# A third seven-product unit in the first output pair of the second MLP product, groups 0 to 2

## The chip, the cores and the metric

The kernel runs on one core of a Trainium2 chip. Its time is the device time of one execution in microseconds (us), as the median of several runs. The engines are TensorE (PE, matrix products; PEld is its weight load), VectorE (DVE), ScalarE (ACT), GpSimd (POOL) and SyncE (SP), which issues the loads of the weights.

## The reference

One encoder layer on 256 tokens with a width of 2048, in float32. The change lies in its last part, the MLP:

```
h2 = rms_norm(x, g_mlp[layer])
x = x + jnp.square(jax.nn.relu(h2 @ w_mlp_in[layer])) @ w_mlp_out[layer]
...
return rms_norm(x, g_final)
```

`w_mlp_in` is 2048 x 8192 and `w_mlp_out` 8192 x 2048. The hidden values are computed and used in four groups (`g` 0 to 3) of 2048 columns.

## The kernel before, in words

**Precision.** Every float32 operand is split into a high part (`whi`, rounded by ScalarE, `high_part`, L637) and a low part (`wlo`, what is left, by VectorE, `low_part`, L1022). One product in float32 is then three products on TensorE: high by high, high by low, low by high (`three_passes`, L1719 to L1721). A *block* is one such pair of parts, made of one piece of weights of 128 x 1024 elements.

**Loads.** SyncE loads the pieces in the order in which they are used (L610) into seven slots in this stage (`raw`, and part of `gates`). A slot is loaded again when the low part of the last block that needs it has been made (`released`).

**A group.** Four strips of hidden values (`hidden`, j = 0 to 3) come out of the first product. Of each, VectorE adds two halves (L1472), takes the maximum with 0 and scales (L1474), ScalarE squares (L938) and rounds to `b_hi` (L941), VectorE makes `b_lo` (L1479). This is done beside TensorE's next window. Then comes the second product, which has four strips of 512 output columns, two at a time: `pair(g, 0)` and `pair(g, 1)` (group 3 has the first pair only). I call them pair 0 and pair 1. A pair runs over four *units* of 512 hidden values, with four pieces each.

**Plain and crossed units.** The hidden values of a unit are 2 x 2 tiles (halves of the tokens by halves of the unit), and so are its weights (halves of the unit by the two strips): eight tile products in a plain unit. A crossed unit does the same with seven products of sums and differences (`seven`, the Winograd form of Strassen's rule). For it VectorE makes four sums of hidden values (`s_sum`, L1485 to L1490), split into `s_hi` (ScalarE, L944) and `s_lo` (VectorE, L1493), once a unit; and four differences of weight pieces (L1025), in place. The seven blocks are b11, b22, t1, b21, t3, t2, t4, in this order; b11, b22 and b21 are pieces as loaded, t1 to t4 differences. So a plain unit has four blocks with 12 products of 512 columns each on TensorE, a crossed one seven blocks with 6 each.

**Which units are crossed.** Before the change: units 1 and 2 in pair 0, units 0, 1 and 2 in pair 1 (`CROSSED`). The sums are there for the hidden strips 0 to 2 (`SUMMED`).

**PSUM.** It has two halves, G and S, with four banks each. In pair 0 the plain units and three of the seven products add up in G (`sums_bank`), the other four of the seven in S (`mix_bank`); in pair 1 it is the other way round. So before pair 1 begins, ScalarE has to copy pair 0's S banks out (`mix_out`, L967, done in the order of its work at step `MIX_OUT` of the pair's second half), and TensorE waits for that (`m_out`). G is copied at the start of pair 1 (`carry_out`, L954).

**What sets the order.** Each engine works through its list in program order. A table written at build time (`DUE`) says at which step of TensorE's pieces each block is split: about seven blocks ahead. High parts also wait until the block eight places back has been used (`slot_free`), low parts for their high part, and TensorE for the low part (`lo_made`).

Of the kernel before, what the change touches and what calls it, by code (L numbers as in the profile page):

```python
# [66 lines left out]
def walk(eng, window):  # L67
# [36 lines left out]
    for g in range(4):  # L104
# [20 lines left out]
PAIR_ORDER = {  # L125
    0: tuple((unit, part) for unit in range(4) for part in range(4)),
    1: ((3, 0), (3, 1), (0, 0), (0, 1), (0, 2), (0, 3), (1, 0), (1, 1), (1, 2), (1, 3), (3, 2), (2, 0), (2, 1), (2, 2),
        (2, 3), (3, 3)),
}
MIX_OUT = {0: 4, 1: 5}  # L130
# [7 lines left out]
def pair_place(n):  # L138

    g, i = divmod(n - N_MLP, 8 * PIECES)  # L140
    if n < N_MLP or i < 4 * PIECES or (g == 3 and i >= 6 * PIECES):
        return None
    q, i = divmod(i - 4 * PIECES, 2 * PIECES)
    return (g, q) + PAIR_ORDER[q][i]


def crossed(n):

    at = pair_place(n)
    return at is not None and at[2] in CROSSED[at[1]]  # L150


def crossed_before(g, q, unit):

    return g * (len(CROSSED[0]) + len(CROSSED[1])) + q * len(CROSSED[0]) + CROSSED[q].index(unit)


def piece_slot(n):
# [103 lines left out]
def build(nc, x, x_t, w_in, w_dt, gains_in, taps_in, rows_in, w_ssm_up, w_attn_up, w_out, w_mlp_in, w_mlp_out,  # L262
# [275 lines left out]

    def pair_done(g, q, unit):

        return BLOCK[N_MLP + 8 * PIECES * g + 4 * PIECES + 2 * PIECES * q + PAIR_ORDER[q].index((unit, 3)) + 1]

    cum_rows = nc.dram_tensor("cum_rows", (2, HEADS, T), F32).ap()

# [87 lines left out]
    def _(act):  # L632
# [294 lines left out]
        def hidden(p, idx, pr, pp):  # L927
            g, j = idx
            if p == 0:
                act.wait_ge(used, done(pr, pp))  # L930
                if g or j > SUMMED[0]:
                    act.wait_ge(s_lo_made, len(SUMMED) * g + sum(u < j for u in SUMMED))
# [9 lines left out]
            if p == 5 and j in SUMMED:  # L942
                act.wait_ge(s_v, 4 * (len(SUMMED) * g + j) + 4)
# [11 lines left out]

        def mix_out(p, idx, pr, pp):
            g, q = idx
            if p != MIX_OUT[q]:
                return
            act.wait_ge(used, pair_done(g, q, CROSSED[q][-1]))  # L960
# [58 lines left out]
    def _(dve):  # L1019
# [445 lines left out]
        def hidden(p, idx, pr, pp):  # L1465
            g, j = idx
            if p == 0:
                dve.wait_ge(hid_t, g * 4 + (j + 1))
                if 4 * g + j:
                    dve.wait_ge(hid_lo, g * 4 + j)  # L1470
                dve.wait_ge(hid_hi, g * 4 + (j + 1))
                dve.tensor_tensor(hidden_u, hidden_t, hidden_banks(j)[:, :, 0:T], ALU.add).then_inc(h_taken, 1)  # L1472
                dve.wait_ge(h_taken, g * 4 + (j + 1))
                dve.scalar_tensor_tensor(out=hidden_u, in0=hidden_u, scalar=0.0,  # L1474
                                         in1=rstd_row[:, :].unsqueeze(1).to_broadcast([P, 4, T]),
                                         op0=ALU.max, op1=ALU.mult).then_inc(hid_v, 1)
            if p == 2:
                dve.wait_ge(hid_hi, g * 4 + (j + 2))
                dve.tensor_tensor(b_lo[:, 4 * j:4 * j + 4, :], hidden_u,  # L1479
                                  b_hi[:, 4 * j:4 * j + 4, :].bitcast(F32), ALU.subtract).then_inc(hid_lo, 1)  # L1480
            if p == 3 and j in SUMMED:
                a11, a12 = hidden_u[:, 0:2, 0:P], hidden_u[:, 2:4, 0:P]
                a21, a22 = hidden_u[:, 0:2, P:T], hidden_u[:, 2:4, P:T]
                turn = 4 * (len(SUMMED) * g + j)
# [6 lines left out]
            if p == 5 and j in SUMMED:  # L1491
                dve.wait_ge(s_hi_made, len(SUMMED) * g + j + 1)
# [220 lines left out]
    def _(pe):  # L1713
# [230 lines left out]
        def seven(block, q, unit, m, start, stop):  # L1944
# [5 lines left out]
            if block in ("b11", "t2", "t3", "t1"):  # L1950
                first_one, last_one = start, stop
            else:
                first_one, last_one = False, (block, q, unit) == ("b22", 1, 2)
# [12 lines left out]
        def pair_window(r, par, idx):  # L1966

            g, q, _ = idx
            turn = 2 * g + q
            for p in range(PIECES):  # L1970
                n = piece_number(r, par, p)
                _, _, unit, part = pair_place(n)
                if (unit, part) == PAIR_ORDER[q][0]:
                    if q:
                        pe.wait_ge(m_out, 2 * turn)
                    else:
                        pe.wait_ge(h_taken, 4 * g + 3)
                        pe.wait_ge(hid_lo, 4 * g + 3)
                if (unit, part) == (CROSSED[q][0], 0):
                    pe.wait_ge(s_lo_made, len(SUMMED) * (g + 1))  # L1980
                    if q:
                        pe.wait_ge(c_out, 2 * (g + 1))
                    else:
                        pe.wait_ge(h_taken, 4 * g + 4)
                if (q, unit, part) == (0, 3, 0):
                    pe.wait_ge(hid_lo, 4 * g + 4)
                if crossed(n):
                    for i in range(2 * part, min(2 * part + 2, len(PAIR_BLOCKS))):
                        pe.wait_ge(lo_made, BLOCK[n] + i + 1)
# [183 lines left out]
```

## Time and profile before

| | us |
|---|---|
| median of 3 runs (1622.16 to 1622.67) | 1622.39 |
| span of the profiled execution, first to last instruction | 1620.0 |
| TensorE busy in it | 1608.5 |
| VectorE busy | 1264.1 |
| ScalarE busy | 917.1 |

The profiled execution is one execution; its rows give durations and the order of events, and its span lies 2.4 us under the median of the runs. An engine's busy time is averaged over stages that differ, so the pairs are to be read by themselves.

### The profile page before, as it was taken

How to read it: one execution, taken by the hardware profiler on the slowest of the kernel's cores; microseconds unless marked ns; L12 is line 12 of the kernel's file. 1: busy time of each engine (PE TensorE's matmuls, PEld its weight loads, DVE VectorE, ACT ScalarE, POOL GpSimd, SP SyncE). 2: the span in 40 equal slices, each digit the busy share in tenths (PEclk: the TensorE clock that was granted, in tenths of full speed). 3: DMA queues.
4: the chain of work that ended last, by engine and by line, in shares of the span. 5: the costliest groups of instructions: out<-in, count | busy, mean ns of one | idle time of the engine just before them, and what ended most of it. 6: DMA issues, size and time to landing. Idle time of an engine off the chain costs nothing.

```text
span 1620.0 us, 20751 instructions
## 1 busy us (share of the span) xinstructions
PE 1608.5 (99%) x8104; PEld 1362.2 (84%) x8104; DVE 1264.1 (78%) x1520; ACT 917.1 (57%) x1262; POOL 79.1 (5%) x67
## 2 busy tenths in 40 slices
PE   9999999999999999999999999999999999999998
PEld 7888888888888888888888888888888888888886
DVE  7888878888666677776665576999799988998893
ACT  6666556666565445544444555665556556655562
POOL 3000000000001134000000000000000000000000
PEclk9999999999999999999999999999999999999999
DMA  7666665666556664445576676458646764586471
GB/s 272 202 200 190 189 200 189 208 195 203 183 186 182 191 187 153 142 145 175 187 229 195 225 236 187 144 182 285 184 125 224 262 190 134 194 282 209 148 245 53
DMA packets 134194, 312.21 MB, mean 193 GB/s; under 512 B 9744, under 2 KB 10448, under 8 KB 133968
## 3 DMA queue, kind: packets, MB, share of 16 engines
q1 hardware_dynamic: 129376, 302.21, 58.4%
q10 hardware_dynamic: 4720, 8.68, 2.0%
q8 instruction: 64, 1.05, 0.3%
q14 instruction: 34, 0.28, 0.0%
HBM read 308.68 MB, written 2.16 MB: 192 GB/s over the span
## 4 chain that ended last, share of the span: by engine, by line
PE 96%; DVE 2%; issue 1%; ACT 0%; POOL 0%; DMA 0%; POOLq 0%; DVEq 0%
PE G L1719 17%; PE G L1720 17%; PE G L1721 17%; PE G L1728 13%; PE S L1728 7%; PE G L1732 6%; PE S L1719 4%; PE S L1721 4%; PE S L1720 4%; PE S L1732 4%; PE S L1740 1%; PE S L1847 1%; DVE wlo L1022 1%; PE S L1891 0%; PE S L1824 0%
## 5 line engine op out<-in xcount | busy, mean ns | idle before, releaser
L637 ACT ACTIVATE whi<-raw 128x1024 fp32r<-128x1024 f32 x395 | 417.0, 1059 | 418.1 <-PE G L1721 254.9
L1022 DVE TENSOR_TENSOR wlo<-raw,whi 128x1024 fp32r<-128x1024 f32 x395 | 482.5, 1236 | 128.7 <-ACT whi L637 127.4
L1719 PE MATMUL G<-whi,a_both 128*128 128x512 f32 x768 | 301.3, 392 | 2.3 <-DVE wlo L1022 1.7
L1721 PE MATMUL G<-whi,a_both 128*128 128x512 f32 x768 | 299.5, 390 | 0.0
L1720 PE MATMUL G<-wlo,a_both 128*128 128x512 f32 x768 | 299.5, 390 | 0.0
L1728 PE MATMUL G<-a_both,whi 128*128 128x512 f32 x640 | 201.7, 397 | 0.0
L1719 PEld LDWEIGHTS G<-whi,a_both 128*128 128x128 f32 x768 | 144.3, 188 | 33.3 <-issue 2.6
L1721 PEld LDWEIGHTS G<-whi,a_both 128*128 128x128 f32 x768 | 144.2, 188 | 30.1
L1720 PEld LDWEIGHTS G<-wlo,a_both 128*128 128x128 f32 x768 | 144.3, 188 | 28.7
L1732 PEld LDWEIGHTS G<-a_both,wlo 128*128 128x128 f32 x640 | 120.3, 188 | 28.2
L1719 PE MATMUL G<-whi,b_hi 128*128 128x512 f32 x342 | 133.9, 392 | 0.0
L1720 PE MATMUL G<-wlo,b_hi 128*128 128x512 f32 x342 | 133.6, 391 | 0.0
L1721 PE MATMUL G<-whi,b_lo 128*128 128x512 f32 x342 | 133.3, 390 | 0.0
L637 ACT ACTIVATE whi_late<-raw 128x1024 fp32r<-128x1024 f32 x85 | 88.9, 1058 | 67.2 <-PE S L1732 22.0
L1732 PE MATMUL G<-a_both,wlo 128*128 128x256 f32 x640 | 125.9, 278 | 0.0
L1022 DVE TENSOR_TENSOR wlo_late<-raw,whi_late 128x1024 fp32r<-128x1024 f32 x85 | 102.6, 1221 | 24.7 <-ACT whi_late L637 24.1
L637 ACT ACTIVATE whi_late<-gates 128x1024 fp32r<-128x1024 f32 x67 | 70.0, 1056 | 49.7 <-PE G L1732 17.9
L1728 PEld LDWEIGHTS G<-a_both,whi 128*128 128x128 f32 x640 | 97.6, 189 | 0.1
L1022 DVE TENSOR_TENSOR wlo_late<-gates,whi_late 128x1024 fp32r<-128x1024 f32 x67 | 81.1, 1221 | 18.7 <-ACT whi_late L637 18.6
L637 ACT ACTIVATE whi<-gates 128x1024 fp32r<-128x1024 f32 x63 | 66.2, 1056 | 38.2 <-PE G L1732 13.9
L1022 DVE TENSOR_TENSOR wlo<-gates,whi 128x1024 fp32r<-128x1024 f32 x63 | 76.3, 1222 | 12.5 <-ACT whi L637 12.0
L1728 PE MATMUL G<-a_both,whi_late 128*128 128x512 f32 x256 | 80.5, 396 | 0.0
(306 smaller groups left out, 2692.4 us busy)
## 6 DMA issues: line engine op xcount, KB each, us to landing
raw<-in_w_in SPq DMA_DIRECT2D x208, 512.0 KB, 4.3
raw<-in_w_mlp_in SPq DMA_DIRECT2D x74, 512.0 KB, 4.0
raw<-in_w_mlp_out SPq DMA_DIRECT2D x74, 512.0 KB, 5.0
gates<-in_w_mlp_in SPq DMA_DIRECT2D x54, 512.0 KB, 4.0
gates<-in_w_mlp_out SPq DMA_DIRECT2D x54, 512.0 KB, 4.9
raw<-in_w_ssm_up SPq DMA_DIRECT2D x32, 512.0 KB, 3.8
raw<-in_w_attn_up SPq DMA_DIRECT2D x32, 512.0 KB, 4.6
raw<-in_w_out SPq DMA_DIRECT2D x32, 512.0 KB, 4.6
```

Of the source, the lines that this page charges most:

```text
L637: act.activation(high(m), piece(n), ACT.Copy).then_inc(hi_made, 1)
L1022: dve.tensor_tensor(low(m), piece(n), high(m).bitcast(F32), ALU.subtract).then_inc(lo_made, 1)
L1719: pe.matmul(out_ap, hi[:, k, cols], w_hi, start=start, stop=False)
L1720: pe.matmul(out_ap, hi[:, k, cols], w_lo, start=False, stop=False)
L1721: return pe.matmul(out_ap, lo[:, k, cols], w_hi, start=False, stop=stop)
L1728: pe.matmul(banks[:, c, :], high(m)[:, cols[kk]], a_both[:, 2 * p + kk, :, :].rearrange("p h t -> p (h t)"), start=(p + kk == 0), stop=False)
L1732: last = pe.matmul(banks[:, c, 0:T], low(m)[:, cols[kk]], a_hi[:, 2 * p + kk, :], start=False, stop=(2 * p + kk == KT - 1))
L1740: last = pe.transpose(S[:, c // 2, c % 2 * T + tb * P:c % 2 * T + (tb + 1) * P], src(c, tb), ident[:, :])
L1847: last = pe.matmul(S[:, 2, (4 * c + h) * HD:(4 * c + h + 1) * HD], mw[:, 0, h, c, :], tm[:, c, h * HD:(h + 1) * HD], start=True, stop=True)
```

## The change

In groups 0 to 2, pair 0 gets a third crossed unit: units 1, 2 and 3, with unit 0 plain. The fourth hidden strip gets its sums, `s_hi` and `s_lo` too; they are put into the scratch tiles `tmp_b` and `tmp_a`. Pair 0's pieces now come in pair 1's pattern: half of the plain unit, two crossed units, a quarter of the plain unit, the third crossed unit, the last quarter. Pair 0's copies (`mix_out`) move from step 4 to step 5 and behind the first split of that step, as in pair 1. Group 3 stays as it was. The core of the diff:

```diff
-CROSSED = {0: (1, 2), 1: (0, 1, 2)}
-SUMMED = (0, 1, 2)
...
+def summed(g):
+    return (0, 1, 2) if g == LAST_GROUP else (0, 1, 2, 3)
...
+def crossed_units(g, q):
+
+    if g == LAST_GROUP:
+        return (1, 2)
+    return (0, 1, 2) if q else (1, 2, 3)
...
+    if g == LAST_GROUP:
+        return whole(0) + whole(1) + whole(2) + whole(3)
+    plain = 3 if q else 0
+    u, v, w = crossed_units(g, q)
+    return ((plain, 0), (plain, 1)) + whole(u) + whole(v) + ((plain, 2),) + whole(w) + ((plain, 3),)
...
+def mix_step(g):
+    return 4 if g == LAST_GROUP else 5
...
-    cut = 1 if at is not None and at[1] == 1 and s % PIECES == MIX_OUT[1] else 0
+    cut = 1 if at is not None and at[0] < LAST_GROUP and s % PIECES == mix_step(at[0]) else 0
...
+    s_hi.append(nc.alloc_sbuf_tensor_at("s_hi3", [P, 4, 2, P], F32R, offset=region_t))
+    s_lo.append(nc.alloc_sbuf_tensor_at("s_lo3", [P, 4, 2, P], F32R, offset=region_t - 4 * TB * N))
...
-            if p == 3 and j in SUMMED:
+            if p == 3 and j in summed(g):
...
-                if (unit, part) == (CROSSED[q][0], 0):
-                    pe.wait_ge(s_lo_made, len(SUMMED) * (g + 1))
+                if (unit, part) == (units[0], 0):
+                    pe.wait_ge(s_lo_made, 4 * g + 3)
...
                 if (q, unit, part) == (0, 3, 0):
                     pe.wait_ge(hid_lo, 4 * g + 4)
+                    if unit in units:
+                        pe.wait_ge(s_lo_made, 4 * g + 4)
```

How it moves the work on VectorE, in pair 0 of group 0, from the addition of the fourth hidden strip on (`tmp_b<-tmp_a,S`). `wlo` and `wlo_late` are low parts, rows that write `raw` or `gates` the differences. Before:

```order
L1472 TENSOR_TENSOR tmp_b<-tmp_a,S 128x1024
L1474 SCALAR_TENSOR_TENSOR tmp_b<-tmp_b,rstd_row 128x1024
L1022 TENSOR_TENSOR wlo<-raw,whi 128x1024 x2
L1479 TENSOR_TENSOR b_lo<-tmp_b,b_hi 128x1024
L1022 TENSOR_TENSOR wlo<-gates,whi 128x1024 x2
L1025 TENSOR_TENSOR gates<-gates 128x1024
L1022 TENSOR_TENSOR wlo_late<-raw,whi_late 128x1024
L1025 TENSOR_TENSOR gates<-raw,gates 128x1024
L1022 TENSOR_TENSOR wlo_late<-gates,whi_late 128x1024
L1025 TENSOR_TENSOR raw<-raw,gates 128x1024
L1022 TENSOR_TENSOR wlo_late<-raw,whi_late 128x1024
```

After (the same operations stand 24 lines lower in the file: L1046 is L1022, L1049 is L1025, L1496 to L1503 are L1472 to L1479), up to the last difference of the pair's second unit:

```order
L1496 TENSOR_TENSOR tmp_b<-tmp_a,S 128x1024
L1498 SCALAR_TENSOR_TENSOR tmp_b<-tmp_b,rstd_row 128x1024
L1046 TENSOR_TENSOR wlo<-raw,whi 128x1024 x2
L1049 TENSOR_TENSOR raw<-gates,raw 128x1024
L1046 TENSOR_TENSOR wlo<-gates,whi 128x1024
L1503 TENSOR_TENSOR b_lo<-tmp_b,b_hi 128x1024
L1049 TENSOR_TENSOR gates<-gates 128x1024
L1046 TENSOR_TENSOR wlo<-raw,whi 128x1024
L1049 TENSOR_TENSOR gates<-gates,raw 128x1024
L1046 TENSOR_TENSOR wlo_late<-gates,whi_late 128x1024
L1049 TENSOR_TENSOR gates<-gates 128x1024
```

and right behind it, with the sums of the fourth strip (L1509 to L1514) and its low part (L1517):

```order
L1509 TENSOR_TENSOR tmp_a<-tmp_b 128x256
L1510 TENSOR_TENSOR tmp_a<-tmp_b 128x256
L1512 TENSOR_TENSOR tmp_a<-tmp_a,tmp_b 128x256
L1514 TENSOR_TENSOR tmp_a<-tmp_b,tmp_a 128x256
L1046 TENSOR_TENSOR wlo_late<-gates,whi_late 128x1024 x3
L1517 TENSOR_TENSOR s_lo_134<-tmp_a,s_hi_133 128x1024
```

The strip's two first operations stood behind the fourth of the first unit's seven blocks and now stand behind the sixth (the two low parts that follow are t3 and t2 before, t4 and the next unit's b11 after); `b_lo` is now among the second unit's blocks. The four sums and `s_lo` are new at this place.

On ScalarE, around its copies of pair 0's S banks (`mt<-S`), with the semaphores that each row waits for (`landed` with a number is the slot of the load). Before:

```order
L637 ACTIVATE whi_late<-gates 128x1024 [waits used,landed6]
L637 ACTIVATE whi_late<-raw 128x1024 [waits used,landed0]
L637 ACTIVATE whi<-raw 128x1024 [waits used,landed1]
L967 ACTIVATE mt<-S 128x1024 [waits used]
L967 ACTIVATE mt<-S 128x1024
L637 ACTIVATE whi<-raw 128x1024 [waits used,landed3]
L637 ACTIVATE whi<-raw 128x1024 [waits used,t_made]
```

After:

```order
L661 ACTIVATE whi<-gates 128x1024 [waits used,landed6]
L661 ACTIVATE whi<-raw 128x1024 [waits used,landed0]
L661 ACTIVATE whi<-raw 128x1024 [waits used,landed1]
L661 ACTIVATE whi_late<-raw 128x1024 [waits used,landed3]
L991 ACTIVATE mt<-S 128x1024 [waits used]
L991 ACTIVATE mt<-S 128x1024
L661 ACTIVATE whi_late<-raw 128x1024 [waits used,t_made]
L661 ACTIVATE whi_late<-gates 128x1024 [waits used,landed4]
```

The high part ahead of the copies was that of b11 of pair 1's first unit (`landed1`) and is now that of its b22 (`landed3`), which came behind the copies before.

## Rows read from the trace of the kernel before

In timelines a row has: start (us from the span's start), duration (of the merged rows together), engine, line, operation, out<-in, shapes, count, and in brackets the idle time before it with what ended it.

**Rows 1.** Page: busy time of an engine, chain that ended last

```profile
PE 1608.5 (99%) x8104; PEld 1362.2 (84%) x8104; DVE 1264.1 (78%) x1520; ACT 917.1 (57%) x1262; POOL 79.1 (5%) x67
PE 96%; DVE 2%; issue 1%; ACT 0%; POOL 0%; DMA 0%; POOLq 0%; DVEq 0%
```

**Rows 2.** Busy time of each engine in pair 0 and pair 1 of group 0

```profile
core 0: us, PE busy (x) PEld busy (x) DVE busy (x) ACT busy (x) POOL busy (x), PEclk, DMA share, GB/s
1019.67:1060.48 40.81, 40.81 (x182) 33.80 (x181) 37.71 (x33) 26.98 (x27) 0.00 (x0) 1.00 0.54 180
1060.48:1099.92 39.44, 39.44 (x175) 32.67 (x174) 37.59 (x33) 26.57 (x27) 0.00 (x0) 1.00 0.60 193
```

**Rows 3.** Timeline of TensorE: where the stretches start, and one block

```profile
1019.67 0.40 PE L1719 MATMUL G<-whi,b_hi 128*128 128x512 f32 x1
...
1060.48 0.39 PE L1719 MATMUL S<-whi_late,b_hi 128*128 128x512 f32 x1
...
1093.12 0.39 PE L1719 MATMUL G<-whi,s_hi 128*128 128x512 f32 x1
...
1099.92 0.39 PE L1728 MATMUL G<-a_both,whi_late 128*128 128x512 f32 x1
```

**Rows 4.** Timeline of VectorE in pair 1 of group 0

```profile
1067.28 1.23 DVE L1022 TENSOR_TENSOR wlo_late<-gates,whi_late 128x1024 fp32r<-128x1024 f32 x1 [1.31 <-ACT whi_late L637]
1068.61 1.23 DVE L1025 TENSOR_TENSOR gates<-gates 128x1024 f32<-128x1024 f32 x1
...
1076.75 1.22 DVE L1022 TENSOR_TENSOR wlo<-gates,whi 128x1024 fp32r<-128x1024 f32 x1
1077.89 4.63 DVE L1022 TENSOR_TENSOR wlo_late<-raw,whi_late 128x1024 fp32r<-128x1024 f32 x4
...
1090.77 1.22 DVE L1022 TENSOR_TENSOR wlo<-gates,whi 128x1024 fp32r<-128x1024 f32 x1
```

**Rows 5.** Timeline of VectorE around the start of pair 0

```profile
1007.10 1.23 DVE L1022 TENSOR_TENSOR wlo<-gates,whi 128x1024 fp32r<-128x1024 f32 x1 [0.31 <-ACT whi L637]
1008.24 0.42 DVE L1485 TENSOR_TENSOR tmp_a<-tmp_b 128x256 f32<-128x256 f32 x1
...
1009.88 1.22 DVE L1022 TENSOR_TENSOR wlo<-raw,whi 128x1024 fp32r<-128x1024 f32 x1
1012.66 1.23 DVE L1022 TENSOR_TENSOR wlo_late<-raw,whi_late 128x1024 fp32r<-128x1024 f32 x1 [1.56 <-ACT whi_late L637]
...
1021.03 1.23 DVE L1022 TENSOR_TENSOR wlo_late<-gates,whi_late 128x1024 fp32r<-128x1024 f32 x1 [0.32 <-ACT whi_late L637]
...
1023.50 1.22 DVE L1472 TENSOR_TENSOR tmp_b<-tmp_a,S 128x1024 f32<-128x1024 f32 x1
1024.75 1.23 DVE L1474 SCALAR_TENSOR_TENSOR tmp_b<-tmp_b,rstd_row 128x1024 f32<-128x1024 f32 x1
```

**Rows 6.** Timeline of ScalarE at the start of pair 0

```profile
1019.93 1.06 ACT L637 ACTIVATE whi_late<-gates 128x1024 fp32r<-128x1024 f32 x1 [1.72 <-PE S L1732]
...
1026.01 1.06 ACT L938 ACTIVATE tmp_b<-tmp_b 128x1024 f32<-128x1024 f32 x1 [2.28 <-DVE tmp_b L1474]
```

**Rows 7.** Timeline of ScalarE around its copies of pair 0's sums

```profile
1046.96 1.06 ACT L637 ACTIVATE whi_late<-gates 128x1024 fp32r<-128x1024 f32 x1 [0.59 <-DMA gates<-in_w_mlp_out]
1050.20 1.06 ACT L637 ACTIVATE whi_late<-raw 128x1024 fp32r<-128x1024 f32 x1 [2.18 <-DMA raw<-in_w_mlp_out]
...
1052.46 1.92 ACT L967 ACTIVATE mt<-S 128x1024 f32<-128x1024 f32 x2
1054.27 2.00 ACT L637 ACTIVATE whi<-raw 128x1024 fp32r<-128x1024 f32 x2
```

**Rows 8.** Timeline of SyncE's queue: issues of weight pieces in pair 0

```profile
1042.64 0.37 SPq L610 DMA_DIRECT2D gates<-in_w_mlp_out  x1
1043.78 0.37 SPq L610 DMA_DIRECT2D raw<-in_w_mlp_out  x1
```

**Rows 9.** Timeline of ScalarE at its copies of pair 1's sums

```profile
1097.40 1.94 ACT L967 ACTIVATE m_acc<-G 128x1024 f32<-128x1024 f32 x2 [0.56 <-PE S L1721]
```

More of the change, by code:

```diff
@@ L122, with pair_order, whole @@
 LATE_RAW = LATE_RING - 1
-CROSSED = {0: (1, 2), 1: (0, 1, 2)}
-SUMMED = (0, 1, 2)
[L125 to L130, printed above, removed]
+LAST_GROUP = 3
+def summed(g):
[4 more added lines that the diff above has]
+    return (0, 1, 2) if q else (1, 2, 3)
+def pair_order(g, q):
+    def whole(unit):
+        return tuple((unit, part) for part in range(4))
+    if g == LAST_GROUP:
[5 more added lines that the diff above has]
+    return 4 if g == LAST_GROUP else 5
 PAIR_PARTS = ((0, 0), (0, 1), (1, 1), (1, 0))
@@ L143, in pair_place @@
     q, i = divmod(i - 4 * PIECES, 2 * PIECES)
-    return (g, q) + PAIR_ORDER[q][i]
+    return (g, q) + pair_order(g, q)[i]
 def crossed(n):
     at = pair_place(n)
-    return at is not None and at[2] in CROSSED[at[1]]
+    return at is not None and at[2] in crossed_units(at[0], at[1])
 def crossed_before(g, q, unit):
-    return g * (len(CROSSED[0]) + len(CROSSED[1])) + q * len(CROSSED[0]) + CROSSED[q].index(unit)
+    return 6 * g + 3 * q + crossed_units(g, q).index(unit)
 def piece_slot(n):
@@ L539, in pair_done @@
     def pair_done(g, q, unit):
-        return BLOCK[N_MLP + 8 * PIECES * g + 4 * PIECES + 2 * PIECES * q + PAIR_ORDER[q].index((unit, 3)) + 1]
+        return BLOCK[N_MLP + 8 * PIECES * g + 4 * PIECES + 2 * PIECES * q + pair_order(g, q).index((unit, 3)) + 1]
     cum_rows = nc.dram_tensor("cum_rows", (2, HEADS, T), F32).ap()
@@ L930, in hidden @@
                 act.wait_ge(used, done(pr, pp))
-                if g or j > SUMMED[0]:
-                    act.wait_ge(s_lo_made, len(SUMMED) * g + sum(u < j for u in SUMMED))
+                if g or j:
+                    act.wait_ge(s_lo_made, 4 * g + j)
                 if g and j == 0:
@@ L941, in hidden @@
                 act.activation(b_hi[:, 4 * j:4 * j + 4, :], hidden_u, ACT.Copy).then_inc(hid_hi, 1)
-            if p == 5 and j in SUMMED:
-                act.wait_ge(s_v, 4 * (len(SUMMED) * g + j) + 4)
+            if p == 5 and j in summed(g):
+                act.wait_ge(s_v, 4 * (4 * g + j) + 4)
                 act.activation(s_hi[j][:, :, :, :], s_sum, ACT.Copy).then_inc(s_hi_made, 1)
@@ L957, in mix_out @@
             g, q = idx
-            if p != MIX_OUT[q]:
+            if p != mix_step(g):
                 return
-            act.wait_ge(used, pair_done(g, q, CROSSED[q][-1]))
+            act.wait_ge(used, pair_done(g, q, crossed_units(g, q)[-1]))
             if g:
@@ L1480, in hidden @@
                                   b_hi[:, 4 * j:4 * j + 4, :].bitcast(F32), ALU.subtract).then_inc(hid_lo, 1)
-            if p == 3 and j in SUMMED:
+            if p == 3 and j in summed(g):
                 a11, a12 = hidden_u[:, 0:2, 0:P], hidden_u[:, 2:4, 0:P]
                 a21, a22 = hidden_u[:, 0:2, P:T], hidden_u[:, 2:4, P:T]
-                turn = 4 * (len(SUMMED) * g + j)
+                turn = 4 * (4 * g + j)
                 dve.tensor_tensor(s_sum[:, 0, :, :], a21, a22, ALU.add).then_inc(s_v, 1)
@@ L1490, in hidden @@
                 dve.tensor_tensor(s_sum[:, 3, :, :], a12, s_sum[:, 1, :, :], ALU.subtract).then_inc(s_v, 1)
-            if p == 5 and j in SUMMED:
-                dve.wait_ge(s_hi_made, len(SUMMED) * g + j + 1)
+            if p == 5 and j in summed(g):
+                dve.wait_ge(s_hi_made, 4 * g + j + 1)
                 dve.tensor_tensor(s_lo[j][:, :, :, :], s_sum, s_hi[j][:, :, :, :].bitcast(F32), ALU.subtract
@@ L1533, in mix_out @@
             g, q = idx
-            if g == 3 and p == MIX_OUT[q]:
+            if g == LAST_GROUP and p == mix_step(g):
                 dve.wait_ge(mix_a, 1)
@@ L1942, in last_window, with seven @@
                 last.then_inc(fin_mm, 1)
-        def seven(block, q, unit, m, start, stop):
+        def seven(block, g, q, unit, m, start, stop):
             a11, a12 = (slice(4 * unit + 2 * i, 4 * unit + 2 * i + 2) for i in range(2))
@@ L1952, in seven @@
             else:
-                first_one, last_one = False, (block, q, unit) == ("b22", 1, 2)
+                first_one, last_one = False, block == "b22" and g != LAST_GROUP and unit == crossed_units(g, q)[-1]
             if block in left:
@@ L1968, in pair_window @@
             g, q, _ = idx
-            turn = 2 * g + q
+            turn, units, order = 2 * g + q, crossed_units(g, q), pair_order(g, q)
             for p in range(PIECES):
@@ L1972, in pair_window @@
                 _, _, unit, part = pair_place(n)
-                if (unit, part) == PAIR_ORDER[q][0]:
+                if (unit, part) == order[0]:
                     if q:
@@ L1989, in pair_window @@
                         pe.wait_ge(lo_made, BLOCK[n] + i + 1)
-                        seven(PAIR_BLOCKS[i], q, unit, BLOCK[n] + i, unit == CROSSED[q][0], unit == CROSSED[q][-1]
-                              ).then_inc(used, 1)
+                        seven(PAIR_BLOCKS[i], g, q, unit, BLOCK[n] + i, unit == units[0], unit == units[-1]).then_inc(used, 1)
                 else:
@@ L1999, in pair_window @@
                             last = three_passes(sums_bank(q, half, tb), k, tb, b_hi, b_lo, high(m)[:, cols],
-                                                low(m)[:, cols], (unit, kk) == (PAIR_ORDER[q][0][0], 0) and kh == 0,
-                                                k == KT - 1 and (q, half, tb) != (1, 1, 0))
+                                                low(m)[:, cols], (unit, kh, kk) == (order[0][0], 0, 0),
+                                                (unit, kh, kk) == (order[-1][0], 1, 1) and (
+                                                    g == LAST_GROUP or (half, tb) != (1, 0)))
                     last.then_inc(used, 1)
```

## The prediction

> **What bounds the kernel now.** I read the page first, then the busy time of each engine in the two pairs of group 0, then the order of events there on TensorE, VectorE and ScalarE, and last the weight transfers. The page shows TensorE busy 99% of the span and nearly alone on the chain that ended last [rows 1]. In both pairs of group 0 it has no gap: busy 40.81 of 40.81 us and 39.44 of 39.44 us, at the full granted clock [rows 2]. So products taken away come off the time, as long as their operands stay in time. VectorE is the engine to watch: busy 37.71 and 37.59 us in the same two stretches, with 3.10 and 1.85 us free.
>
> Pair 0 starts on TensorE at 1019.67, pair 1 at 1060.48, the next group at 1099.92 [rows 3]. Pair 0 has 180 products, so one costs 40.81 / 180 = 0.2267 us (the 0.39 us of a row is pipelined). A plain block (12 products) is 2.72 us of TensorE, a block of a crossed unit (6) 1.36 us, a crossed unit of seven 9.52 us.
>
> On VectorE, operations of this size start (4.63 - 1.22) / 3 = 1.14 us apart when nothing holds them [rows 4] (1.135 from one row to the next). A crossed unit is seven low parts and four differences. In pair 1 the first block of a unit starts at 1067.28, the fifth (t3) at 1076.75 and the seventh one 1.14 us after the row of 1077.89 starts; the plain block behind the unit follows at 1077.89 + 2 x 1.137 = 1080.16 [rows 4]. That is 12.88 us for a unit that TensorE does in 9.52 us: each crossed unit costs VectorE 3.36 us of its lead, and inside a unit the worst point is t3, 9.47 us after the first block's start where TensorE is there after 5.44. A plain block gives back 2.72 - 1.14 = 1.59 us. Before the change two units in pair 0 and three in pair 1 are paid from a lead of seven blocks, and at the end it is nearly gone: the low part of t3 in pair 1's last unit ends at 1090.77 + 1.22 = 1091.99 [rows 4], TensorE takes it at 1093.12 [rows 3], 1.13 us later.
>
> **The change, part by part.** *Removed:* in groups 0 to 2, six products of pair 0 each: 6 x 0.2267 = 1.36 us a group, 4.08 us in all. *Added on VectorE a group:* three low parts and four differences for the third unit, the four quarter-size sums of the fourth strip (1009.88 - 1008.24 = 1.64 us [rows 5]) and its s_lo: 8 x 1.135 + 1.64 = 10.7 us. *Added on ScalarE:* three high parts and s_hi, about 4 us; it is busy 26.98 of 40.81 us [rows 2], so that is hidden. *Transfers:* the same 16 pieces a pair, so no price but their times, below. *Order:* pair 0 becomes plain, unit, unit, plain, unit, plain, so its last crossed unit ends one plain block ahead of pair 1.
>
> Where VectorE stands then, on the clock of group 0. The low part of pair 0's eighth block starts at 1021.03 before and, I take it, after, since its high part starts when TensorE has left the first product (1019.93 [rows 6], TensorE at 1019.67 [rows 3]). More work stands ahead of it now, but from the third block's low part at 1007.10 [rows 5] VectorE has 13.9 us and needs 10 x 1.135 + 1.64 = 13.0; it used to idle there (1.56 us at 1012.66 [rows 5]). Behind it come the fourth strip's two operations (they took 1.25 and 1.14 us [rows 5]) from 1022.17, the unit's last low part at 1024.56, and the second unit's first. That one waits for a high part, which on ScalarE now stands behind the square of the fourth strip (it starts when the second operation has ended, as at 1026.01 in [rows 6]): 1024.68, high part 1025.65, low part 1026.75. From here on VectorE has no idle time:
> - second unit plus b_lo (1.14), the four sums (1.64) and s_lo (1.14): 26.75 + 12.88 + 3.92 = 43.55 for the plain block, 44.69 for the third unit;
> - 44.69 + 12.88 = 57.57 plain, then 58.71 and 59.84 (pair 1's plain blocks), 60.97 first unit, 73.85 second, 86.73 plain, 87.87 third; its t3 starts 9.47 later, 97.34, and ends at 1098.56.
>
> TensorE without a wait: pair 0's first unit starts at 1019.67 + 5.44 = 1025.12, the second at 34.64, the third at 46.88, pair 1 at 59.12, its units at 64.56, 74.08 and 86.32, and t3 of the last at 91.76. VectorE's lateness at t3 is then 3.1 us in pair 0's third unit (55.38 against 52.32), 1.7, 5.0 and 6.8 us in pair 1's three. The lateness is a running maximum, not a sum: TensorE waits 6.8 us a group in all.
>
> To that comes a wait of ScalarE's. The copies of pair 0's sums out of PSUM (L967) stood behind b11 of pair 1's first unit, and were done 6 us before pair 1 wanted the banks (start 1052.46, two of them, next high part at 1054.27 [rows 7]; pair 1 at 1060.48). Now they stand behind b22 of pair 1's first unit, whose weights are loaded into a slot that t2 of pair 0's third unit sets free, at 55.30 + 1.22 = 1056.52. It is the third piece of a burst with the same spacing as one before the change, where the third was issued at 1043.78 [rows 8] and used at 1050.20 after a DMA wait of 2.18 us [rows 7]: 6.4 us. So it lands at 1062.9, its high part ends at 1064.0, its low part starts at 1064.05, 0.6 us later than VectorE wanted it (60.97 + 1.33 + 1.14 = 63.44); the two copies run from 63.9, the next high part from 65.75 to 66.8, and that low part slips another 0.5 us. Lateness at the end: 6.8 + 1.15 = 7.95 us. TensorE is kept out of pair 1 until the copies end at 65.9, 6.8 us behind its unhindered 59.12; less than the 7.95 that it waits for anyhow. At the same place of pair 1 the copies start 0.56 us after ScalarE is free (1097.40 [rows 9]), which was early enough.
>
> The sum a group: -1.36 + 7.95 = +6.6 us. After pair 1 the low parts regain 1.6 us a block and the next pair meets a full lead again, so three groups are alike: +19.8 us. The profiled execution spans 1620.0 us, the median of the runs is 1622.39, 2.4 more; I add the difference to the median: 1642.2.
>
> The bounds of the landing: if it took 4.3 us (the piece before it was issued at 1042.64 [rows 8] and used at 1046.96 [rows 7]), the wait vanishes: 6.8 - 1.36 = 5.4 a group, 1638.7. At the other end 1 us more on landing and copies each gives 8.6 a group, 1648. Half a microsecond of handover between engines that my sum may have missed or counted twice is 1.5 us over three groups.
>
> **The rule weighed.** TensorE will now stand idle for about 3.7 us in one piece, between the end of pair 0 (1062.2 with its 3.1 us of waits) and 1065.9; in [rows 2] it never idles and its granted clock is 1.00. The Trainium skill ("TensorE: Matmul & The Clock Gate", section "Why this matters for your kernels") says that idle gaps of that order between bursts of matmuls send the engine back to the lower of its two clock levels. No stretch here shows such a gap, so by the rows the clock stays, and by the rule the result would be that of the third rival below.
>
> **The rivals.**
> 1. *The lead covers it* (other side): if the low parts stayed in time, the time falls by 4.1 us to 1618.3. For it: before the change VectorE is never late, and starts pair 0 sixteen microseconds ahead. Against it: only 1.13 us are left at the end [rows 3, 4] and 10.7 us are added. It decides the sign if less than 1.36 us of lateness is left a group, that is, if some 5.4 us of the 6.8 vanish. 4 in 100; something near a tie, 2 in 100.
> 2. *The waits add up*: if ScalarE, held by copies and landings, also holds back VectorE for the whole idle of TensorE, 3.7 us come on top of the 6.8: +9.1 a group, 1649.8. For it: ScalarE handles b22, the copies and three more high parts in a row there. Against it: VectorE has differences to do meanwhile. 10 in 100.
> 3. *The clock falls*: TensorE goes on after its longest idle time at the lower of the two levels, 1.2 GHz, where each product costs another 0.2267 us. If that lasts over pair 1's two plain blocks and first unit (66 products), it is 15.0 us more; TensorE, already 6.8 late, is then 21.8 late, past VectorE's 7.95, so the group costs 21.8 - 1.4 = 20.4 us, and the time is about 1684. Nothing speaks for or against it in the trace: the granted clock is 1.00 [rows 2], with no such gap. 6 in 100.
>
> **How the numbers follow.** VectorE late, with the landing between its bounds, has 78 in 100 and the range 1636 to 1648; it gives the predicted 1642. Slower holds this and rivals 2 and 3: 94; within 0.2% (3.2 us, about what a measurement of this kernel can tell) 2; faster 4. The range goes to 1649 to take in part of rival 2.
>
> **What would show it.** Right: TensorE has gaps ahead of the first of the three passes (L1743 there), ended by VectorE's low parts, in t3 of pair 0's third and of pair 1's second and third units, with the largest (about 3.7 us) at pair 1's start, ended by ScalarE's copies; VectorE has almost no idle time in the 70 us from 1027; group 3 as before. Wrong: TensorE without gaps (rival 1); granted clock under 1.00 in pair 1 (rival 3); VectorE idle on ScalarE while TensorE waits (rival 2); or low parts at another spacing than 1.135 us.

## The result, and the profile after

The changed kernel takes 1644.11 us (median of 4 runs, 1642.07 to 1644.62), the kernel before 1622.41 us (1622.16 to 1622.67): 21.7 us more, a ratio of 1.0131 with a 95% interval of 1.0119 to 1.0143. The profiled execution spans 1642.5 us. The page's row of busy times and its chain of work that ended last, to be read beside [rows 1]:

```profile
PE 1615.4 (98%) x8086; PEld 1361.5 (83%) x8086; DVE 1295.5 (79%) x1556; ACT 928.9 (57%) x1274; POOL 79.1 (5%) x67
PE 87%; DVE 8%; DMA 2%; issue 1%; ACT 1%; POOL 0%; POOLq 0%; DVEq 0%; ACTq 0%
```

TensorE has lost its cover: VectorE has 8% of the chain (2% before) and DMA 2%. TensorE's own waits, where [rows 1 to 3] had none in this stage (us in total, times, longest):

```profile
PE S L1743 <- ACT mt L991: 9.7, 3, 3.7
PE S L1743 <- DVE wlo_late L1046: 1.6, 2, 0.8
PE G L1743 <- DVE wlo_late L1046: 1.2, 2, 0.6
PE G L1743 <- DVE wlo L1046: 0.9, 3, 0.6
PE S L1743 <- DVE wlo L1046: 0.8, 1, 0.8
```

The longest single wait, 3.7 us, is for ScalarE's copies of pair 0's sums; VectorE's four rows are 4.5 us together. The view counts idle time from the end of the product before. Products overlap, so a wait shows smaller there than the delay of the next start (2.60 us in the view where the start came 2.77 us late); below, losses are read from starts. The busy times of group 0, cut at pair 1's start and at the first block of its first crossed unit:

```profile
core 0: us, PE busy (x) PEld busy (x) DVE busy (x) ACT busy (x) POOL busy (x), PEclk, DMA share, GB/s
1020.46:1065.73 45.27, 40.97 (x176) 32.09 (x174) 42.88 (x41) 28.11 (x29) 0.00 (x0) 1.00 0.54 169
1065.73:1072.93 7.20, 7.20 (x25) 5.76 (x25) 6.83 (x7) 6.62 (x7) 0.00 (x0) 0.76 0.39 141
1072.93:1106.93 34.00, 34.00 (x152) 28.18 (x150) 33.58 (x30) 22.69 (x23) 0.00 (x0) 1.00 0.62 203
```

Pair 0 took 45.27 us, of which 39.45 us are products (174 of 0.2267 us): 5.8 us of waits. The two plain blocks ahead of pair 1's first unit took 7.20 us where 24 products are 5.44, with no idle time and a mean granted clock of 0.76. The rest of pair 1, 34.00 us for 150 products, has no wait at all. The group took 86.47 us from pair 0's start to the next group; it was 80.25 [rows 3]. TensorE's timeline shows the wait and the lower clock one behind the other:

```profile
1020.46 0.40 PE L1743 MATMUL G<-whi,b_hi 128*128 128x512 f32 x1
...
1062.74 0.39 PE L1745 MATMUL G<-whi,b_lo 128*128 128x512 f32 x1
1065.73 0.51 PE L1743 MATMUL S<-whi,b_hi 128*128 128x512 f32 x1 [2.60 <-ACT mt L991]
...
1067.93 0.63 PE L1743 MATMUL S<-whi,b_hi 128*128 128x512 f32 x1
1068.36 0.63 PE L1744 MATMUL S<-wlo,b_hi 128*128 128x512 f32 x1
...
1100.13 0.39 PE L1743 MATMUL G<-whi_late,s_hi 128*128 128x512 f32 x1
```

The last product of pair 0 starts at 1062.74, the first of pair 1 at 1065.73, held by ScalarE's copies. A few products on, they start 0.43 us apart instead of 0.23: the lower clock level. The same two blocks in groups 1 and 2:

```profile
1242.46:1249.67 7.21, 7.21 (x24) 5.76 (x25) 6.70 (x7) 6.62 (x7) 0.00 (x0) 0.76 0.33 112
1418.88:1427.21 8.33, 8.33 (x24) 6.64 (x25) 7.82 (x8) 6.62 (x7) 0.00 (x0) 0.64 0.37 123
```

So in the three groups they took 7.20, 7.21 and 8.33 us, at 0.76, 0.76 and 0.64 of the clock. VectorE and ScalarE at the places that the prediction named:

```profile
1021.81 1.22 DVE L1046 TENSOR_TENSOR wlo_late<-raw,whi_late 128x1024 fp32r<-128x1024 f32 x1 [0.83 <-ACT whi_late L661]
...
1027.54 1.23 DVE L1046 TENSOR_TENSOR wlo<-raw,whi 128x1024 fp32r<-128x1024 f32 x1 [0.98 <-ACT whi L661]
...
1055.90 1.22 DVE L1046 TENSOR_TENSOR wlo_late<-raw,whi_late 128x1024 fp32r<-128x1024 f32 x1
...
1098.30 1.22 DVE L1046 TENSOR_TENSOR wlo_late<-gates,whi_late 128x1024 fp32r<-128x1024 f32 x1
```

```profile
1057.74 1.99 ACT L661 ACTIVATE whi<-raw 128x1024 fp32r<-128x1024 f32 x2
1062.80 1.06 ACT L661 ACTIVATE whi_late<-raw 128x1024 fp32r<-128x1024 f32 x1 [3.07 <-DMA raw<-in_w_mlp_out]
1063.76 1.92 ACT L991 ACTIVATE mt<-S 128x1024 f32<-128x1024 f32 x2
1065.57 1.06 ACT L661 ACTIVATE whi_late<-raw 128x1024 fp32r<-128x1024 f32 x1
```

Pair 0 starts 0.79 us later in this execution (1020.46 against 1019.67), so 0.79 is taken off to compare. The eighth low part is at 1021.02 (21.03 predicted), the second unit's first at 1026.75 (26.75), t3 of pair 1's last unit at 1097.51 (97.34). ScalarE waited 3.07 us for b22's weights and started its high part at 1062.01 (62.9 predicted).

That is group 0. In groups 1 and 2 VectorE idled longer for ScalarE's high parts at the start of pair 1: 0.90 + 0.41 = 1.31 us and 0.52 + 0.41 + 0.54 = 1.47 us, where group 0 has 0.27. The rows of group 1:

```profile
1240.61 1.22 DVE L1046 TENSOR_TENSOR wlo_late<-gates,whi_late 128x1024 fp32r<-128x1024 f32 x1 [0.90 <-ACT whi_late L661]
1243.39 1.23 DVE L1046 TENSOR_TENSOR wlo_late<-raw,whi_late 128x1024 fp32r<-128x1024 f32 x1 [0.41 <-ACT whi_late L661]
```

The low part of t3 in pair 1's last unit was ready 0.61, 0.64 and 1.13 us before TensorE took it (groups 0 to 2). In the kernel before it was 1.13 us in all three.

### The profile page after: what moved, and what is told of

It reads as the page before. It is cut to its first block, busy times and chain, and to the rows that moved or that the text cites. A ratio compares the mean times of both kernels' runs of the same rounds, so it can differ in the third digit from the quotient of the medians.

```text
span 1642.5 us, 20778 instructions
## 1 busy us (share of the span) xinstructions
PE 1615.4 (98%) x8086; PEld 1361.5 (83%) x8086; DVE 1295.5 (79%) x1556; ACT 928.9 (57%) x1274; POOL 79.1 (5%) x67
## 4 chain that ended last, share of the span: by engine, by line
PE 87%; DVE 8%; DMA 2%; issue 1%; ACT 1%; POOL 0%; POOLq 0%; DVEq 0%; ACTq 0%
PE G L1743 15%; PE G L1744 15%; PE G L1745 15%; PE G L1752 13%; PE S L1752 7%; PE G L1756 6%; PE S L1756 4%; PE S L1743 3%; PE S L1744 3%; PE S L1745 3%; DVE wlo L1046 2%; DVE wlo_late L1046 2%; DVE gates L1049 1%; PE S L1764 1%; PE S L1871 1%
## 5 line engine op out<-in xcount | busy, mean ns | idle before, releaser
L661 ACT ACTIVATE whi<-raw 128x1024 fp32r<-128x1024 f32 x407 | 429.1, 1059 | 421.5 <-PE G L1745 250.2
L1046 DVE TENSOR_TENSOR wlo<-raw,whi 128x1024 fp32r<-128x1024 f32 x407 | 498.2, 1239 | 126.0 <-ACT whi L661 125.2
L1743 PE MATMUL G<-whi,b_hi 128*128 128x512 f32 x322 | 126.5, 393 | 0.9 <-DVE wlo L1046 0.9
L1744 PE MATMUL G<-wlo,b_hi 128*128 128x512 f32 x322 | 125.8, 391 | 0.0
L1745 PE MATMUL G<-whi,b_lo 128*128 128x512 f32 x322 | 125.5, 390 | 0.0
L661 ACT ACTIVATE whi_late<-raw 128x1024 fp32r<-128x1024 f32 x77 | 80.5, 1057 | 66.7 <-PE S L1756 22.5
L661 ACT ACTIVATE whi_late<-gates 128x1024 fp32r<-128x1024 f32 x79 | 83.0, 1057 | 60.7 <-PE G L1756 20.8
L1046 DVE TENSOR_TENSOR wlo_late<-raw,whi_late 128x1024 fp32r<-128x1024 f32 x77 | 93.1, 1221 | 21.9 <-ACT whi_late L661 21.5
L1046 DVE TENSOR_TENSOR wlo_late<-gates,whi_late 128x1024 fp32r<-128x1024 f32 x79 | 95.5, 1220 | 12.4 <-ACT whi_late L661 12.0
L1752 PE MATMUL S<-a_both,whi 128*128 128x512 f32 x256 | 80.5, 396 | 0.0
```

The costliest lines, as they stand in the source:

```text
L661: act.activation(high(m), piece(n), ACT.Copy).then_inc(hi_made, 1)
L1046: dve.tensor_tensor(low(m), piece(n), high(m).bitcast(F32), ALU.subtract).then_inc(lo_made, 1)
L1743: pe.matmul(out_ap, hi[:, k, cols], w_hi, start=start, stop=False)
L1744: pe.matmul(out_ap, hi[:, k, cols], w_lo, start=False, stop=False)
L1745: return pe.matmul(out_ap, lo[:, k, cols], w_hi, start=False, stop=stop)
L1752: pe.matmul(banks[:, c, :], high(m)[:, cols[kk]], a_both[:, 2 * p + kk, :, :].rearrange("p h t -> p (h t)"), start=(p + kk == 0), stop=False)
```

## The experiments

Two readings stood against each other. **D**: VectorE's work in the two pairs sets the time; the other waits only decide where TensorE stands. **W**: the wait for the copies and the lower clock behind it are the loss, and VectorE's work would fit. Each run was timed beside the kernel before on the same chip; that kernel took 1622.03 to 1622.23 us there, so times of different runs can be compared to about 0.2 us.

**The copies first.** ScalarE copies pair 0's sums ahead of b22's high part.

```diff
-    cut = 1 if at is not None and at[0] < LAST_GROUP and s % PIECES == mix_step(at[0]) else 0
+    cut = 1 if at is not None and at[1] == 1 and at[0] < LAST_GROUP and s % PIECES == mix_step(at[0]) else 0
```

> The changed kernel, with ScalarE's copies of pair 0's sums put ahead of b22's high part (one cut less in the step's list). Theory D (VectorE's work in the two pairs sets the time, the rest only decides where TensorE waits): VectorE's lateness stays at some 6.8 to 7 us a group less 1.36, so 1638.5 to 1641 us, TensorE's waits move from pair 1's start into its second and third unit. Theory W (the wait for the copies and the lower clock behind it are the loss, VectorE's work would fit): 9.7 us of waits and some 5 us of lower clock go, 1629 to 1631 us. Both expect no granted clock under 1.00 in pair 1.

Measured: 1639.25 us, ratio 1.0106 (1.0091 to 1.0121). TensorE's waits:

```profile
PE G L1743 <- issue: 4.6, 3, 1.9
PE G L1743 <- DVE wlo L1046: 3.7, 7, 0.8
PE S L1743 <- DVE wlo_late L1046: 1.9, 3, 0.8
PE G L1743 <- DVE wlo_late L1046: 1.9, 3, 0.7
PE S L1743 <- DVE wlo L1046: 1.2, 2, 0.8
```

The waits for the copies of the S banks (9.7 us) are gone, but only 4.9 us of time with them. By the traces the three groups took 86.74, 86.36 and 86.08 us, where the changed kernel has 86.47, 87.59 and 88.38: group 0 gained nothing. The spans of the two traces differ by 4.2 us, and 0.95 of these lie ahead of pair 0 of group 0. VectorE's rows rose from 4.5 to 8.7 us, and a new wait of 1.5 us a group stands ahead of pair 1's first crossed unit ("issue" in the row). There the code waits for ScalarE's other copies (`c_out`), and those come out of ScalarE only now: they stand behind a high part that waited 0.53 us for one of VectorE's differences, start at 1067.50, and TensorE goes on at 1069.52. So this wait too is VectorE's lateness, handed on by ScalarE. In every group the last wait is for the low part of t3 in pair 1's last unit. The time lies in D's range and 8 us above W's. But both had expected the clock to stay, and in group 0 the level fell here too, behind a wait of 1.87 us:

```profile
1069.52 0.47 PE L1743 MATMUL G<-whi,b_hi 128*128 128x512 f32 x1 [1.87 <-issue]
...
1070.52 0.42 PE L1744 MATMUL G<-wlo,b_hi 128*128 128x512 f32 x1
1070.75 0.62 PE L1745 MATMUL G<-whi,b_lo 128*128 128x512 f32 x1
1071.17 0.63 PE L1743 MATMUL S<-whi_late,s_hi 128*128 128x512 f32 x1
```

**Differences cut short.** The four differences of pair 0's third unit are done for 8 columns instead of 1024, so the kernel leaves out nearly all of them, and that unit's products are not the reference's.

```diff
+            cols = slice(0, 8) if unit == (0, 3) else slice(0, 2 * N)
+            dve.tensor_tensor(piece(n)[:, cols], piece(of)[:, cols], piece(less)[:, cols], ALU.subtract
```

> The changed kernel, with the four differences of pair 0's third unit done for 8 of 1024 columns (that unit's products are then not the reference's; TensorE's, ScalarE's and the transfers' work stays as it is). VectorE has some 4 us less to do a group. Theory D: lateness falls by about 4 us a group in pair 0's third unit and in pair 1; b22's weights land that much earlier, so the copies wait less too: 1630 to 1633 us. Theory W: pair 1's start is earlier by the landing alone, 1632 to 1636. It tells the size of VectorE's share rather than the two apart.

Measured: 1628.87 us, ratio 1.0041 (1.0026 to 1.0056), a little better than either reading said. TensorE's waits:

```profile
PE S L1745 <- ACT mt L991: 4.3, 3, 1.6
PE G L1745 <- DVE wlo L1046: 2.0, 4, 0.8
PE G L1745 <- DVE wlo_late L1046: 1.0, 2, 0.8
```

The cut difference takes 0.09 us of VectorE's list instead of 1.135, so VectorE has 4.2 us less to do a group. The time fell by 15.2 us, 5.1 a group. The waits for the copies are shorter (1.6 us at most, where they were 3.7), the granted clock did not fall, and the last wait of each group is again for VectorE. So some 4.2 us are VectorE's work, and most of the rest is what TensorE had lain behind VectorE's limit in the changed kernel (0.6 to 1.1 us a group, see the 0.61 to 1.13 us above).

**Both edits.** The copies first, and the differences cut short.

> Both edits of e1 and e2 in the changed kernel: the copies ahead of b22, and the four differences of pair 0's third unit cut to 8 columns (its products are then not the reference's). Theory D: e2 still ended with TensorE waiting for VectorE in pair 1, so putting the copies first moves the waits and takes little off: 1627 to 1629 us, beside 1628.9 of e2. Theory W: e2's 4.3 us of waits for the copies go, 1624.5 us.

Measured: 1629.62 us, ratio 1.0047 (1.0032 to 1.0062); no better than 1628.87. The 4.3 us of waits for the copies went, and TensorE waited for VectorE instead:

```profile
PE G L1745 <- DVE wlo L1046: 3.1, 6, 0.8
PE G L1745 <- DVE wlo_late L1046: 1.4, 2, 0.8
PE S L1745 <- DVE wlo_late L1046: 0.7, 2, 0.4
```

W would have had 1624.5. The clock did not fall, no wait for ScalarE is over 0.2 us, and the last wait of every group is for VectorE: here VectorE alone sets the time.

**The order alone.** Pair 0 in the new order, its unit 3 plain as before, so that no engine has more work.

```diff
-    return (0, 1, 2) if q else (1, 2, 3)
+    return (0, 1, 2) if q else (1, 2)
...
-    u, v, w = crossed_units(g, q)
+    u, v, w = (0, 1, 2) if q else (1, 2, 3)
```

> The change's order of pieces and its place of the copies in pair 0, with two crossed units as before (units 1 and 2; unit 3 plain, in the third unit's place). No operation more than before on any engine. Theory D: 1622 to 1623 us, since VectorE has the work of before. Theory W (the order and the copies' place cost): more than 1626 us.

Measured: 1622.18 us, ratio 1.0000 (0.9991 to 1.0010), and the trace has no wait of TensorE in the whole stage. Neither the order nor the copies' place costs anything by itself, as long as VectorE has the work of before.

**More work for VectorE in the kernel before**, eight operations a group in pair 0's last unit, and then four.

```diff
+                    for _ in range(2):
...
+                        dve.tensor_tensor(g_last[:, 2 * N * half:2 * N * (half + 1)], piece(n), high(m).bitcast(F32),
+                                          ALU.subtract).then_inc(extra, 1)
```

> The kernel before, with eight more VectorE operations of 128x1024 in pair 0's last unit of groups 0 to 2, written to a tile that nobody reads (9.1 us a group); nothing else is changed. Theory D: less the 1.13 us of margin and some 2.3 us of idle time, lateness 5.7 us a group, 1639 to 1640 us. Theory W: the work fits in, 1622 to 1624 us.

Measured: 1638.35 us, ratio 1.0100 (1.0085 to 1.0115). TensorE's longest waits:

```profile
PE G L1732 <- issue: 4.5, 3, 1.5
PE G L1732 <- DVE wlo L1023: 4.4, 7, 0.8
```

The first row is again the wait for the copies of the G banks, 1.51 us in each group; ScalarE makes them behind a high part that waits for VectorE. The last wait of each group is for VectorE's t3, and the clock did not fall. Then the half dose (`range(1)`):

> The kernel before with four unread VectorE operations in pair 0's last unit (4.5 us a group) where e4 had eight (9.1 us, 1638.35 us). If past a margin every microsecond of VectorE is a microsecond of the time, the four operations taken off give back 3 x 4.54 = 13.6 us: 1624.7 us. If VectorE's load acts in another way (contention, say), about half of e4's rise: 1630 us.

Measured: 1624.52 us, ratio 1.0016 (1.0006 to 1.0026). Its waits:

```profile
PE G L1732 <- DVE wlo L1023: 1.5, 3, 0.5
```

Each time is taken against the kernel before of its own round: 2.49 us more for the first 4.54 us of VectorE's work a group, 16.12 us more for twice that. So the first 4.54 us cost 0.83 us a group and the next 4.54 us cost (16.12 - 2.49) / 3 = 4.54. Up to some 3.7 us a group the work is hidden; above that, each microsecond costs a microsecond. The change's 10.7 us are 7.0 us over it. Less the 1.36 us of products that is 5.6 us a group, some 1639 us in all (an estimate; the work stands at another place of the list), and the run with the copies first measured 1639.25.

**GpSimd for the fourth difference**, in all crossed units of the changed kernel.

```diff
-                difference(n + 3, n + 3, n + 2)
...
+            pool.wait_ge(t_made, 3 * turn + 3)
+            pool.wait_ge(lo_made, m + 1)
+            pool.tensor_tensor(piece(n), piece(n), piece(n - 1), ALU.subtract).then_inc(t4_made, 1)
```

> The changed kernel, with the fourth difference of every crossed unit (t4) made by GpSimd instead of VectorE. VectorE has six operations (6.8 us) a group less. If GpSimd works beside it, theory D gives little or no lateness: 1618 to 1624 us, which may beat both kernels. Rival: VectorE and GpSimd hold each other up when both read two operands from SBUF, so VectorE gains nothing or loses: 1642 us and more, with VectorE's low parts behind a GpSimd operation longer than 1.22 us.

Measured: 1667.53 us, ratio 1.0280 (1.0264 to 1.0295). GpSimd's operations, and VectorE's at the same times:

```profile
1017.65 2.39 POOL L1733 TENSOR_TENSOR raw<-raw 128x1024 f32<-128x1024 f32 x1 [72.84 <-DVE wlo_late L1053]
1036.23 3.12 POOL L1733 TENSOR_TENSOR gates<-gates 128x1024 f32<-128x1024 f32 x1 [16.19 <-DVE wlo_late L1053]
1053.59 4.38 POOL L1733 TENSOR_TENSOR gates<-gates,raw 128x1024 f32<-128x1024 f32 x1 [14.24 <-DVE wlo_late L1053]
```

```profile
1018.01 4.24 DVE L1053 TENSOR_TENSOR wlo_late<-raw,whi_late 128x1024 fp32r<-128x1024 f32 x2 [0.51 <-ACT whi_late L665]
...
1037.12 2.51 DVE L1517 TENSOR_TENSOR tmp_a<-tmp_b,tmp_a 128x256 f32<-128x256 f32 x1
...
1059.09 1.23 DVE L1053 TENSOR_TENSOR wlo_late<-gates,whi_late 128x1024 fp32r<-128x1024 f32 x1 [3.37 <-ACT whi_late L665]
```

Two low parts that take 2.35 us elsewhere take 4.24 beside the first, and a sum of 0.42 us takes 2.51 beside the second; the third lasts 4.38 us, and VectorE then idles 3.37 us for the high part that waits for it. In the first two cases VectorE ends when it would have ended had it started behind GpSimd (1020.04 + 2.35 = 1022.39 and 1039.35 + 0.42 = 1039.77, measured 1022.25 and 1039.63), and in the third GpSimd ends 2.25 us after VectorE's two low parts, about the 2.39 us that it takes alone. The two don't work side by side. That is what the Trainium skill says ("SBUF — State Buffer", section "SBUF: two separate sides"): an operation of VectorE with two operands from SBUF and one of GpSimd that reads SBUF exclude each other for a whole instruction. The granted clock fell too, twice in each group, each time by a wait of 2.5 us. The control, the same edit in the kernel before:

> The kernel before, with the same fourth differences on GpSimd: the control for it. If GpSimd works beside VectorE, no change (1622 us, TensorE has no waits to lose). If they hold each other up, VectorE's margin of 1.13 us is used up and the time rises, above 1626 us.

Measured: 1636.35 us, ratio 1.0086 (1.0069 to 1.0103), with TensorE's waits

```profile
PE S L1734 <- DVE wlo_late L1029: 5.4, 3, 2.5
PE S L1734 <- DVE wlo L1029: 3.7, 3, 2.5
```

Its clock fell behind two of its three longest waits. So less work on VectorE's list is not enough if it goes to GpSimd. Only the fourth difference was moved; whether another piece of VectorE's work, or the same one at another time, would fit on GpSimd was not tried.

**Two crossed units in pair 1.** D and the trace of the changed kernel disagree on one thing: in the trace nothing in pair 1 waits for VectorE. So pair 1's third unit was made plain.

```diff
-    return (0, 1, 2) if q else (1, 2, 3)
+    return (0, 1) if q else (1, 2, 3)
```

> The changed kernel's pair 0, with pair 1 cut to two crossed units (its unit 2 is plain, in the same place): TensorE has as many products a group as in the kernel before, VectorE 8 us less than in the changed kernel. If VectorE's total over both pairs sets the time (my prediction's reading), nearly all of pair 1's lateness goes: some 3 us a group stay, 1632 us. If the waits ahead of pair 1 and the lower clock behind them set it by themselves, as the changed kernel's trace has it (5.8 to 6.9 us of waits and 1.8 to 2.9 us of clock a group), the time doesn't fall: 1622.4 + 25.8 less what the clock varies, 1645 to 1648 us.

Measured: 1645.07 us, ratio 1.0141 (1.0126 to 1.0156), as the changed kernel. With 8 us a group less for VectorE the time stayed. TensorE has its 18 products (4.1 us) back in this run, so what it loses is 23.0 us, where the changed kernel loses 21.7 + 4.1 = 25.8. Inside pair 1 it waits for nothing. The waits up to pair 1's start and the lower clock are thus enough by themselves for nearly all of the loss. They vary: by the trace the groups took 87.81, 90.54 and 85.77 us, 7.6, 10.3 and 5.5 us over the 80.25 of before. The wait for the copies:

```profile
PE S L1743 <- ACT mt L991: 9.4, 3, 4.5
```

and the clock was at 0.79 of full speed over the 16 us around pair 1's start in group 1 (0.89 in group 0 over 15 us, and 1.00 in group 2).

**Two crossed units in pair 1, and the copies first.**

> The same with the copies ahead of b22. Then both causes are gone but for VectorE's lateness in pair 0's third unit (3.1 us a group) and the wait for the copies of the G banks that the run with the copies first showed (1.5 us a group): 1622.4 + 9 to 14, 1631 to 1636 us.

Measured: 1638.60 us, ratio 1.0102 (1.0087 to 1.0117), above what was expected. TensorE's waits:

```profile
PE G L1743 <- issue: 4.2, 3, 1.7
PE G L1743 <- DVE wlo_late L1046: 2.6, 6, 0.6
```

The waits for the G copies and for VectorE in pair 0 were foreseen. Beside them this trace has another 0.8 us a group in pair 1, where the low parts of its second crossed unit are late again; that term I had left out. The clock did not fall. TensorE's waits are 5.8, 5.0 and 5.9 us in the three groups, where the run with the copies first and all crossed units has 7.9, 7.5 and 7.2: VectorE's 8 us in pair 1 were worth some 1.9 us of waits a group there, of which the products that come back take 1.36, so the two runs differ by little (1638.60 and 1639.25).

## Why the prediction was right

**The sign and the size.** 1642.2 was forecast, 1644.11 came, inside the range. The products saved are real (8086 on TensorE for 8104). TensorE's loss in a group was forecast as 7.95 us of waits and measured, with the lower clock in it, as 7.58, 8.70 and 9.49 us in groups 0 to 2 (the groups take 86.47, 87.59 and 88.38 us, of which 78.89 are the 348 products). Less the 1.36 saved, 6.2, 7.3 and 8.1 us a group are 21.7 us; the rest of the span's 22.5 us (0.8) came ahead of pair 0.

**VectorE's list, step by step.** Without the 1.15 us that I added for ScalarE's hold, its starts held within 0.2 us over 76 us in group 0. Its wait in pair 0's third unit was forecast as 3.1 us; TensorE lost 3.06 us up to that unit's end. Where TensorE waits for a low part it starts some 0.05 us behind its end, so the 0.61, 0.64 and 1.13 us by which t3 was early put VectorE's own lateness at 7.0, 8.1 and 8.4 us a group. The forecast was 6.8 us plus what ScalarE holds VectorE back by. With the idle times that VectorE's rows show around pair 1's start the sum comes out in both kernels:

| | VectorE idle, us | 6.8 plus that | lateness measured |
|---|---|---|---|
| changed kernel, groups 0, 1, 2 | 0.27, 1.31, 1.47 | 7.1, 8.1, 8.3 | 7.0, 8.1, 8.4 |
| copies first, groups 0, 1, 2 | 0.98, 0.64, 0.32 | 7.8, 7.4, 7.1 | 7.9, 7.5, 7.2 |

**The copies behind b22.** Right, with a landing of 5.6 us in group 0 where I took 6.4. TensorE waited 2.6, 3.7 and 3.4 us for the copies where I had 3.7, and in all 5.8, 6.9 and 6.6 us up to pair 1's start where I had 6.8.

**The step that failed: "less than the 7.95 that it waits for anyhow".** I let VectorE's lateness in pair 1 decide the end, 6.8 us and another 1.15. The 1.15 came as 0.27, 1.31 and 1.47 us, but TensorE never met it: in pair 1 it waits for no low part. What I had put at nothing in the sum was the clock, and it cost 1.8 us in groups 0 and 1 and 2.9 in group 2, which put TensorE 0.6, 0.6 and 1.1 us behind VectorE's limit. That is rival 3 in its mechanism, at a far smaller size. Of the signs that I had named, the gaps in t3 of pair 1's second and third units did not appear, and one sign of being wrong did, the granted clock under 1.00 in pair 1. I had it last over 66 products; the rows show it for some 8 to 13, and TensorE was back at full speed ahead of the first crossed unit. The rule that I weighed (the Trainium skill, "TensorE: Matmul & The Clock Gate", section "Why this matters for your kernels") held in all three groups: each gap, 2.6 to 3.7 us, came with the lower level. "Nothing speaks for or against it in the trace" was a miss: in the kernel before TensorE's last product starts at 1612.02, and the mean granted clock of 1610 to 1620 us is 0.79. That the number came out near is in part luck: the clock's 6.4 us fell where TensorE would otherwise have waited for VectorE, so they added only some 2.2 us to the 23.5 of VectorE's lateness.

The two limits are seen apart when one is taken away. Without the copies' wait VectorE takes over, at 1639.25; without VectorE's third crossed unit in pair 1 the waits ahead of it stay, at 1645.07. Both limits have one root: the copies are late because b22's weights are, these wait for a slot that VectorE's low part of t2 sets free, and with 4.2 us less for VectorE in pair 0 the wait for the copies fell from 9.7 to 4.3 us.

**Rival 1** (the lead covers it) is out: the margin is some 3.7 us of VectorE's work a group and the change adds 10.7. **Rival 2** (the waits add up over VectorE's) came in part: in group 1 VectorE idled 0.90 us for a high part while TensorE stood in its longest wait (1238.7 to 1242.5). With 0.27 to 1.47 us a group it stayed near the 1.15 of my own sum and far below the 3.7 of the rival.

**Not settled:** why the lower clock lasts longer in group 2, and what decides after a wait of some 2 us: the level fell behind one of 1.87 us in the run with the copies first and not behind one of 2.1 us in group 2 of the run with two crossed units in pair 1. No run takes away the lower clock alone. No version tried beats the kernel before.

## What to carry to other kernels

A kernel whose matrix engine is 99% busy can still be one step from another engine's limit. Write down, for each engine that feeds it, how early its last result is ready at the tightest place (1.13 us here), and price any work added to that engine against this margin, in the order of its list, before counting what the matrix engine saves. Trading 6 products (1.36 us) for 10.7 us of VectorE's work can't pay where VectorE has some 3.7 us to spare, and taking away the largest wait gave back 4.9 us where it had been 9.7, for VectorE's limit lay right below. When two limits lie within a microsecond, take away each alone and then both: the trace names only the one that came last. And look at every group: the first one had less of ScalarE's hold on VectorE and less of the lower clock than the last.

## What the runs showed of the hardware

Whether TensorE's clock fell by a wait, from the granted clock around every wait of over 1 us in groups 0 to 2 of all traces:

| wait of TensorE, us | how many | lower level came with it |
|---|---|---|
| 2.60 to 4.46 | 5 | 5 |
| 2.46 to 2.51 | 9 | 8 |
| 1.97 to 2.15 | 4 | 0 |
| 1.87 | 1 | 1 |
| 1.21 to 1.75 | 10 | 0 |

At the lower level products start 0.43 us apart instead of 0.23. In the changed kernel TensorE went on at it for some 8 to 13 products and was back at full speed without another wait. The one of 2.46 to 2.51 us without it is in group 1 of the kernel before with GpSimd's differences. A wait of 1.87 us came with the lower level where four longer ones did not, so the length of the wait is not all that decides; what else does, no run shows.

GpSimd and VectorE operations with two operands in SBUF exclude each other: a difference of 128 x 1024 elements takes GpSimd 2.4 us alone and up to 4.4 us beside VectorE, and VectorE's operation beside it is longer by 1.9 to 2.1 us.
